# The conv gate's sigmoid, moved from an activation on ScalarE to an exponential there and a sum and a reciprocal on VectorE

## The reference

```python
proj = rms_norm(x, attn_norm_w) @ w_in          # split into q, k, v, u (2 x 1024 channels), g
q, k = rms_norm(q), rms_norm(k)                 # per head, 64 dimensions
p = softmax(q1 k1 + bias) - lam * softmax(q2 k2 + bias)      # 8 heads, blocks of 128 queries, causal
a = p @ v                                       # then a norm with a gain
u_a, u_b = split(u)                             # 1024 channels each
c = causal_depthwise_conv(u_a * sigmoid(u_b), conv_w, conv_b)   # 31 taps per channel
```

## Time and profile before

| | us |
|---|---|
| median of the runs | 3425.42 |
| the profiled execution | 3416.88 |
| its span, first to last instruction | 3414.8 |
| PE busy | 2963.5 (87%) |
| DVE busy | 1568.8 (46%) |
| ACT busy | 1232.4 (36%) |
| POOL busy | 719.9 (21%) |

### The profile page before, as it was taken

One profiled execution on the slowest core, in us unless ns is written; L12 is line 12 of the kernel. 1 busy time (PEld: TensorE's weight loads), 2 busy tenths in 40 slices (PEclk: granted clock), 3 DMA queues, 4 the chain that ended last, 5 costly groups with the idle time before them and its releaser, 6 DMA issues. The chain is left out here.

```text
span 3414.8 us, 35302 instructions
## 1 busy us (share of the span) xinstructions
PE 2963.5 (87%) x13448; PEld 2387.7 (70%) x13448; DVE 1568.8 (46%) x1931; ACT 1232.4 (36%) x2003; POOL 719.9 (21%) x317
## 2 busy tenths in 40 slices
PE   6999998877778769988998899693985989998998
PEld 5787886656667657776777678481874878787786
DVE  3666652346763146777877776414222210111121
ACT  3555542334531245555555555423113110111110
POOL 2111121110002112332233323123211121121111
PEclk8999999989999979999999999896998999999999
DMA  4112122132224122121112212241420111111112
GB/s 110 44 44 62 56 74 62 24 62 46 49 100 147 37 77 59 54 62 51 58 45 64 62 54 84 99 129 56 147 93 20 48 37 50 48 45 43 43 43 74
DMA packets 239268, 218.87 MB, mean 64 GB/s; under 512 B 29304, under 2 KB 200856, under 8 KB 239128
## 3 DMA queue, kind: packets, MB, share of 16 engines
q1 hardware_dynamic: 238096, 215.41, 20.5%
q10 hardware_dynamic: 1032, 1.57, 0.3%
HBM read 156.66 MB, written 41.42 MB: 58 GB/s over the span
## 5 line engine op out<-in xcount | busy, mean ns | idle before, releaser
L179 POOL TENSOR_TENSOR w_lo<-w_raw,w_hi 128x1024 fp32r<-128x1024 f32 (+3 forms) x228 | 539.1, 2366 | 2119.2 <-ACT w_hi L171 2119.2
L171 ACT ACTIVATE w_hi<-w_raw 128x1024 fp32r<-128x1024 f32 (+3 forms) x228 | 224.0, 985 | 789.0 <-PE u_y_ps L1763 222.3
L197 PE MATMUL d_pp<-h_hi,w_hi 128*128 128x512 f32 x896 | 366.4, 409 | 33.6 <-DVE d_padded L2424 21.6
L2402 DVE SCALAR_TENSOR_TENSOR d_acc<-d_padded,vectors,d_acc 128x1024 f32<-128x1024 f32 x240 | 388.1, 1617 | 3.6
L197 PE MATMUL d_pp<-h_hi,w_lo 128*128 128x512 f32 x896 | 364.9, 407 | 0.0
L197 PE MATMUL d_pp<-h_lo,w_hi 128*128 128x512 f32 x896 | 362.3, 404 | 0.0
L197 PEld LDWEIGHTS d_pp<-h_hi,w_hi 128*128 128x128 f32 x896 | 172.1, 192 | 81.1 <-issue 25.3
L197 PE MATMUL s_pp<-h_hi,w_hi 128*128 128x512 f32 x512 | 205.9, 402 | 12.9 <-PEq L67 12.9
L2182 POOL TENSOR_TENSOR d_probs<-d_probs 128x128 f32<-128x128 f32 (+3 forms) x64 | 129.7, 2026 | 383.0 <-ACT d_probs L2298 383.0
L197 PE MATMUL s_pp<-h_hi,w_lo 128*128 128x512 f32 x512 | 204.7, 400 | 0.0
L197 PE MATMUL s_pp<-h_lo,w_hi 128*128 128x512 f32 x512 | 203.7, 398 | 0.0
(11 more groups left out here) (336 smaller groups left out, 6499.8 us busy)
## 6 DMA issues: line engine op xcount, KB each, us to landing
w_raw<-in_w_in SPq DMA_DIRECT2D x97, 512.0 KB, 3.8
w_raw<-in_w_gate_up SPq DMA_DIRECT2D x44, 512.0 KB, 3.8
w_raw<-in_w_down SPq DMA_DIRECT2D x22, 512.0 KB, 3.7
gates<-s_gate SPq DMA_DIRECT2D x16, 512.0 KB, 5.1
f_gate<-gates SPq DMA_DIRECT2D x16, 512.0 KB, 4.6
w_raw<-in_w_out SPq DMA_DIRECT2D x16, 512.0 KB, 3.6
w_raw<-in_w_proj SPq DMA_DIRECT2D x16, 512.0 KB, 4.8
x_tok_in<-in_x SPq DMA_DIRECT2D x8, 512.0 KB, 8.0
```

The costliest lines, as they stand in the source:

```text
L171: act.activation(self.hi[:, s, 0:chunks, :], self.raw[:, s, 0:chunks, :], ACT.Copy).then_inc(self.rounded[s], 1)
L179: pool.tensor_tensor(self.lo[:, s, 0:chunks, :], self.raw[:, s, 0:chunks, :], f32(self.hi[:, s, 0:chunks, :]), ALU.subtract).then_inc(self ...
L197: mm = pe.matmul(halves(ps)[h], w[:, k, :], x[:, k, h * HALF:(h + 1) * HALF], start=(k == 0 and r == 0), stop=(k == chunks - 1 and r == 2))
L2402: dve.scalar_tensor_tensor(out=acc[:, :], in0=x, scalar=wt, in1=acc[:, :], op0=ALU.mult, op1=ALU.add).then_inc(c["taps"], 1)
```

## The change

The second table set is no longer used in the stage. `take` of a tile b makes exp(-u_b) of each half straight from PSUM. DVE then adds 1 and takes the reciprocal, half by half, with a semaphore between the two (`plus_one`), and `feed_conv` waits for both halves. On DVE the new function `sigmoid` stands where the half of b ends, in the same place of the part as `feed_conv`. The planner counts 1.0 us of DVE work for each half of b, and so deals the taps out a little differently.

```diff
-            load += sum(0.7 for t, e in halves_in(s, x) if stream[t][0] == "a")
+            load += sum({"a": 0.7, "b": 1.0}.get(stream[t][0], 0) for t, e in halves_in(s, x))
...
-                    act.activation(sig[:, cut], pp[:, cut], ACT.Copy).then_inc(c["taken_b"], 1)
+                    act.activation(sig[:, cut], pp[:, cut], ACT.Exp, scale=-1.0).then_inc(c["taken_b"], 1)
...
-                if h == 1 and what == "b":
-                    act.preload_act_table_set("sigmoid_and_others")
-                    act.wait_ge(c["taken_b"], 2 * (n + 1))
-                    act.activation(sig[:, :], sig[:, :], ACT.Sigmoid).then_inc(c["sigmoids"], 1)
-                    act.preload_act_table_set("natural_log_exp_and_others")
...
+            def sigmoid(t, e):
+
+                h = stream[t][1]
+                cut = slice(e * HALF, (e + 1) * HALF)
+                dve.wait_ge(c["taken_b"], 2 * h + e + 1)
+                dve.tensor_scalar(sig[:, cut], sig[:, cut], 1.0, None, ALU.add).then_inc(c["plus_one"], 1)
+                dve.wait_ge(c["plus_one"], 2 * h + e + 1)
+                dve.reciprocal(sig[:, cut], sig[:, cut]).then_inc(c["sigmoids"], 1)
...
-                    dve.wait_ge(c["sigmoids"], h + 1)
+                    dve.wait_ge(c["sigmoids"], 2 * (h + 1))
...
             dve.wait_ge(c["pad_zero"], 1)
+            for e in range(2):
+                sigmoid(0, e)
             for e in range(2):
                 feed_conv(1, e)
...
                         for t, e in halves_in(s, x):
+                            if stream[t][0] == "b":
+                                sigmoid(t, e)
                             if stream[t][0] == "a":
                                 feed_conv(t, e)
```

More of the change, by code:

```diff
@@ L1999, in differential_and_conv @@
         upper = [sc[:, i, HALF:TOK] for i in range(2)]
-        names = """taken_q taken_k taken_v taken_b sigmoids conv_in gate_done squared summed logged inverted normed q_round
+        names = """taken_q taken_k taken_v taken_b plus_one sigmoids conv_in gate_done squared summed logged inverted normed q_round
             q_low k_round k_low v_turned v_round v_low scored biased maxed prob weighted scaled mixed turned
```

## The result

The changed kernel takes 3460.48 us in the median of four runs (3459.34 to 3466.38), against 3425.78 us for the kernel before on the same chips. The ratio is 1.0106, with a 95% interval of 1.0088 to 1.0123: 1.1% slower, about 35 us. The forecast was 3450, so the direction and the place were right, and the added time (24.5 us where some 35 were measured) was three tenths too small.

The account below looks back on a forecast made before the run. PE was taken to bound the kernel, with DVE next at 79% in the stage. Heads 0 to 4 (23.5 us) plus heads 5 and 6 (1 us) on the median 3425.4 gave 3450 us; range 3424 to 3468.

Parts of the forecast that it names:

- rival 4: DVE's reciprocal is dearer, 4.5 us and a pair with the sum 5.0; 3460 us, with the clock's bound 3468; chance 0.20.
- The price of the reciprocal: On DVE, a 128x512 reciprocal takes 3.3 us, from a slope of 6.2 ns per element in small rows.
- rival 1: DVE's reciprocal costs nearly any wide operation's price, a pair with the sum 1.0 us; -1 in all, 3424 us; chance 0.10.
- The sum: On DVE, adding 1 to each 128x512 half of b takes 0.45 us.
- Heads 0 to 4: Late row maximum of b = 4 makes PE 4.7 us late in each of five heads, 23.5 us.
- The cover of the first pair: In heads 0 to 4, DVE's 2.91 us wait for k's norm hides the first half's sum and reciprocal, leaving 0.9 us.
- Heads 5 and 6: Pairs of sum and reciprocal against removed table loads add 1 us in both heads together; bounds: gain 5.7, loss 6.
- Taps: The planner's new 1.0 us moves single taps between neighbouring parts of a head; cost 0, within 1 us per head.
- The clock: PE's longer stall could bring more time at 1.2 GHz; taken as 0, at most 8 us over five heads.
- The start: The second half of b0's pair ends at 1258.0, before a0's first product can start at 1259.29; cost 0.
- Rival 2: ACT's relief decides: 11 us of PE's waits go and DVE takes the pairs in idle time; 3414 us; chance 0.08.
- Rival 3: Half the lateness is made up as DVE's later waits in a head shrink; +12 us, 3437; chance 0.17.

Follow-up runs that it names:

- relief_only: The kernel before with both table loads and the sigmoid left out of ACT for each tile b, nothing added on DVE; 3421.54 us, ratio 0.9993.
- sums_only: The changed kernel with the taps dealt out as before and all wide reciprocals left out, the sums kept; 3424.61 us, ratio 0.9998.
- old_deal: The changed kernel with the planner's line of the kernel before, so the taps are dealt out as before; 3450.77 us, ratio 1.0072.
- first_free: old_deal with the reciprocals of the first halves alone left out (8 of 16), the sum kept; 3444.55 us, ratio 1.0056.
- second_free: old_deal with the reciprocals of the second halves alone left out (8 of 16), the sum kept; 3435.27 us, ratio 1.0023.
- second_late_old_deal: old_deal with the second half's sum and reciprocal moved right ahead of the feed of a's first half; 3450.53 us, ratio 1.0073.
- deal_only: The kernel before with nothing but the planner's new term, 1.0 us for each half of b; 3432.02 us, ratio 1.0024.

## Why the prediction was right, and where its size was off

The time of 3460.48 us lies inside the stated range of 3424 to 3468, but outside the 3441 to 3458 that the forecast kept for its own account. It lies on the number of rival 4, 3460, whose cause (a reciprocal of 4.5 us) the row of 3.354 us rules out. So the direction and the main chain were right: a dear reciprocal, uncovered in the second half, makes the row maximum of b = 4 late, and PE stands for it. Most of the 10 us above 3450 is the new deal of the taps, 8.6 us of head time.

A ladder of single edits, in sums of head times, splits the 33.1 us. Its first three steps together land on the prediction's sum:

| step | us | predicted |
|---|---|---|
| ACT's relief (before to relief_only) | -6.0 | in the terms below |
| 16 sums (to sums_only) | +3.2 | in the terms below |
| 16 reciprocals (to old_deal) | +27.3 | in the terms below |
| together, the old deal of taps | +24.5 | +24.5 |
| the new deal (to after) | +8.6 | 0 |
| all | +33.1 | +24.5 |

By the ratios of whole times the four steps are about -2, +2, +25 and +12 us, each ratio uncertain by 3 to 6 us. They show the two large steps; the two small ones rest on the stage's lengths alone.

*The price of the reciprocal* (3.3 us) held at 3.354, so 6.3 ns per element: (3354 - 155) / 511. The slope from two to eight elements was the right one. Rival 4 falls with it, and rival 1. The Trainium skill, "VectorE: DVE Perf Modes", section "First, the fixed hardware budget", has a repeat count of 8 for the reciprocal; read as eight cycles per element at that page's clock of 0.96 GHz, it gives an estimated 4.3 us. The measurement decides: the page points the right way, and the estimate from it is a quarter too high.

*The sum* (0.45 us) is 0.42 where it runs alone, and was not priced for company: 2.6 us beside POOL in heads 1 to 4. That cost only 0.4 us a head there, since it took the place of a tap that had paid the same; in head 0 it was the tap behind the sum that paid (sums_only).

*Heads 0 to 4* (4.7 each): 4.3 in heads 1 to 4. The cover of the first pair and the bare second one are shown by first_free and second_free. The step was right in size and too narrow in its reason. I had put the loss down to one point without slack. second_late_old_deal shows that the place ahead of a's feed has no slack either. Head 0, at 3.9 with the old deal, is not taken apart further than by sums_only.

*Heads 5 and 6* (+1 together): +3.7 with the old deal (2.1 and 1.6), within the bounds given. With the 20.8 of heads 0 to 4 (predicted 23.5) this makes the 24.5, so the exact agreement of the sums is luck: two errors of 2.7 us, of opposite sign.

*Taps, price 0, kept to 1 us per head*: this step failed. It is +8.6 us, head 5's 7.5 and head 0's 2.7, less 2.1 in head 6. I had looked at where taps move ahead of b = 4 in heads 0 and 1 and called the moves behind it neutral. In head 5 a G tile is read out just behind b = 6's exponentials, which no row of my argument looked at: deal_only shows its wait at 4.02 us in place of 1.09. The runs do not take head 0's 2.7 us apart.

*The clock, price 0 and at most 8 us*: PE's busy time of the stage rose by 15.3 us for the same matmuls, at 0.95 of full speed in place of 0.98. This is a share of the head times above, not a term on top. No run changed the clock alone, so how much of it DVE would have cost PE in any case is not separated. deal_only shows both kinds: 1.7 us that were paid behind the wait of b = 6, and 2.9 us of busy time more in b = 3 and 4 that lengthened the stretch by 0.4. Whether the bound of 8 us was too low stays open.

*The start* (cost 0): a0's feed was not delayed by the pair; the distance from PE's first matmul to the first feed is 19.5 us before and 19.9 after.

*Rival 2*, ACT's relief deciding, has at most 6.0 us of 11 behind it (relief_only) and is outweighed. The prediction's list of PE's waits on ACT left one out: 8.1 us on the squares for norms, L2247. Relief did not shorten it (9.7 us in relief_only), so no term was lost by it:

```profile
PE d_sc L2576 <- ACT d_probs L2247: 8.1, 10, 1.2
```

*Rival 3*, half made up again, did not happen: heads 1 to 4 kept what they lost.

## What to carry to other kernels

Before work is moved from an engine with room to one that is nearly full, price the operation by the slope of its small rows, not by the class of instruction it seems to belong to. Rows of two and eight elements per partition gave 6.2 ns per element, where the sum's two gave 2.7, and the wide ones took 3.35 us against 0.42. This is one operation of one chip: a slope from so small rows can be off elsewhere. Where a planner's estimate changes with the edit, run the new plan on the old kernel by itself; a quarter of this loss was the plan. And when two engines take turns as the bound, moving added work to "a place with slack" can move the wait only, as it did here. What helped was a form of the work that adds nothing to the full engine: two more activations from the table set already loaded, 0.15% faster than before, where the form on DVE was 1.1% slower.

## What the runs showed of the hardware that was not expected

A DVE sum of 128x512 with an immediate takes 0.42 us alone and up to 2.63 us beside POOL's subtraction. In head 1 of the changed kernel it started at 1487.68 and ended at 1490.31, and POOL's subtraction ended 0.3 us before that:

```profile
1486.81 3.21 POOL L179 TENSOR_TENSOR w_lo<-w_raw,w_hi 128x1024 fp32r<-128x1024 f32 x1 [6.81 <-ACT w_hi L171]
```

In second_late_old_deal, where no sum meets such a subtraction, the mean of the same 16 sums is 419 ns. What decides is which of the two starts second. A tap (128x1024, two inputs) takes 1.28 us alone. In the kernel before, 74 taps started more than 0.1 us into a POOL instruction, and all of them ended 1.08 to 1.14 us behind its end, whatever that made their length; the six such sums after ended 0.28 to 0.29 us behind it. The tap of 3.47 us in sums_only is one that started with POOL's (1371.23 + 3.47 is 1.08 us behind 1371.22 + 2.40). In relief_only it started 0.33 us ahead of POOL's and kept its 1.28. So where a short DVE instruction of these kinds starts against POOL's counts for more than how long it is alone. The reciprocal's 3.35 us never varied by more than 3 ns (3352 to 3355), beside POOL or not.
